# Gate and residual folded into the output accumulation, the final norm read from PSUM, and both scatters of the former pair ahead of the transposes

## The reference, cut to what matters

```python
    for l in range(DEPTH):
        ...
        h = rms_norm(x, ffn_norm_g[l]) * (1.0 + scale_f) + shift_f
        ffn = moe_ffn(h, ...)          # routed experts + shared expert
        x = x + gate_f * ffn
    return rms_norm(x, final_norm_g)

    # in moe_ffn, per chunk of tokens:
        a = jnp.einsum('td,edf->tef', tc, w1)
        b = jnp.einsum('td,edf->tef', tc, w3)
        hid = jax.nn.silu(a) * b * gc[:, :, None].astype(tc.dtype)
        return jnp.einsum('tef,efd->td', hid, w2)
    shared = jnp.einsum('tf,fd->td', jax.nn.silu(t @ sw1) * (t @ sw3), sw2)
```

## Time and profile before

| | us |
|---|---|
| median of 3 runs | 802.24 |
| lowest and highest | 800.73, 805.15 |
| the profiled execution | 803.2 |
| its span, first to last instruction | 801.4 |
| PE busy, of the span | 731.0 (91%) |
| DVE busy | 284.4 (35%) |
| ACT busy | 175.5 (22%) |
| HBM read and written | 269.51 MB and 1.05 MB |

### The profile page before, as it was taken

How to read it: one execution, slowest core, us unless ns; L and a number is a source line. 1 busy time by engine, 2 the same in 40 slices (tenths; PEclk the granted TensorE clock), 3 DMA queues, 4 the chain that set the end, 5 groups by cost and what they waited for, 6 DMA issues and landing times.

```text
span 801.4 us, 12516 instructions
## 1 busy us (share of the span) xinstructions
PE 731.0 (91%) x5004; PEld 384.2 (48%) x5004; DVE 284.4 (35%) x750; ACT 175.5 (22%) x351; POOL 10.6 (1%) x25
## 2 busy tenths in 40 slices
PE   4699999999998988999997999999999997999991
PEld 1478888888885444333332333333333333333330
DVE  1118493855546484212221222221222222222225
ACT  3213320200000333212121212121212222212122
POOL 0200001000000010000000000000000000000000
PEclk9899999999999999999999999999999999999996
DMA  9999526695959253999999999999999999999951
GB/s 337 372 340 366 171 95 220 227 326 174 359 208 421 85 236 123 422 422 420 421 420 418 422 420 422 420 421 395 413 418 422 419 421 419 421 420 421 420 216 52
DMA packets 73429, 271.37 MB, mean 339 GB/s; under 512 B 4424, under 2 KB 33232, under 8 KB 48416
## 3 DMA queue, kind: packets, MB, share of 16 engines
q1 hardware_dynamic: 71664, 264.26, 84.0%
q0 software_dynamic: 1408, 6.20, 2.0%
q10 hardware_dynamic: 304, 0.13, 0.1%
HBM read 269.51 MB, written 1.05 MB: 338 GB/s over the span
## 4 chain that ended last, share of the span: by engine, by line
PE 81%; DVE 9%; ACT 3%; DMA 3%; issue 2%; SPq 2%; DVEq 0%; ACTq 0%
PE bank L1087 78%; DVE slot_gate L1034 2%; PE bank L1398 2%; DVE reg L1038 2%; DMA ring<-ada_w_dram 2%; DVE reg L1029 2%; ACT reg L618 2%; SPq L356 1%; DMA reg<-reg 1%; ACT h_hT L603 0%; DVE x_sb L1070 0%; DVE part L1069 0%; DVE part L738 0%; DVE h_hT L1078 0%; ACT h_hT L646 0%
## 5 line engine op out<-in xcount | busy, mean ns | idle before, releaser
L1087 PE MATMUL bank<-ring,h_hT 128*32 128x512 f32 (+2 forms) x2144 | 256.3, 590 | 7.4 <-issue 7.4
L1087 PEld LDWEIGHTS bank<-ring,h_hT 128*32 128x32 f32 (+1 forms) x2144 | 84.5, 114 | 169.2 <-issue 167.5
L1087 PE MATMUL bank<-h_hT,ring 128*128 128x256 f32 x704 | 157.6, 383 | 1.8 <-ACT h_hT L464 1.8
L1087 PEld LDWEIGHTS bank<-h_hT,ring 128*128 128x128 f32 x704 | 135.0, 192 | 21.3 <-ACT h_hT L464 2.2
L1087 PE MATMUL bank<-ring,turned 128*32 128x512 f32 x1024 | 116.5, 595 | 0.0
L1029 DVE TENSOR_TENSOR reg<-reg,bank 128x256 f32<-128x256 f32 x32 | 13.5, 421 | 212.9 <-ACT reg L618 212.9
L1050 DVE TENSOR_TENSOR y_part<-bank,y_part 128x512 fp32r<-128x512 f32 x64 | 44.2, 691 | 123.9 <-ACT y_part L629 91.1
L1087 PEld LDWEIGHTS bank<-ring,turned 128*32 128x32 f32 x1024 | 30.0, 109 | 69.1 <-issue 69.1
L618 ACT ACTIVATE reg<-bank 128x256 f32<-128x256 f32 x32 | 12.3, 384 | 220.3 <-PE bank L1087 220.3
L1087 PE MATMUL bank<-y_part,give 64*128 64x512 f32 (+1 forms) x268 | 49.4, 443 | 2.3 <-DVE y_part L1050 1.5
L1087 PE MATMUL bank<-take,h_part 128*128 128x256 f32 x288 | 50.6, 300 | 0.7 <-ACT h_hT L603 0.7
(11 more groups left out here) (221 smaller groups left out, 415.6 us busy)
## 6 DMA issues: line engine op xcount, KB each, us to landing
ring<-exp_w_dram SPq DMA_DIRECT2D x192, 1024.0 KB, 13.0
ring<-ada_w_dram SPq DMA_DIRECT2D x24, 1024.0 KB, 12.1
ring<-w_in_dram SPq DMA_DIRECT2D x24, 1024.0 KB, 12.8
ring<-w_branch_dram SPq DMA_DIRECT2D x4, 1024.0 KB, 12.4
ring<-w_out_dram SPq DMA_DIRECT2D x4, 1024.0 KB, 8.1
ring<-shared_w_dram SPq DMA_DIRECT2D x2, 1024.0 KB, 13.8
reg<-ada_bp_dram POOLq DMA_DIRECT2D x3, 512.0 KB, 8.6
x_sb<-x_dram SPq DMA_DIRECT2D x1, 1024.0 KB, 5.3
```

What stands on the lines that cost most here:

```text
L1087: return pe.matmul(o, lhsT, rhs, start=start, stop=stop, skip_group_check=True)
```

## The change

Three things are done.

1. **The gate.** `gate_f` is multiplied into the shared expert's w2 once, on DVE ahead of the loop (two operations of 128 x 1024), and into y of each pair, on DVE, in place in banks 6 and 7 (two operations of 128 x 512 a pair), before ACT copies it. ACT now waits for that (`y_gated`).
2. **The residual and the norm.** Four matmuls of the identity with `x_sb`, between the two loops, add x into the output banks. Behind the loop ACT squares the output banks themselves (with the factor 1/32 inside the square, so that the mean needs no further multiply), and DVE scales from the banks. The eight DVE operations of gate and residual are gone, and one of the three small ones of each norm. A root of one unused column is put on ACT right behind the loop, ahead of the squares.
3. **The scatters.** `scatter(1 - r, 1)` now stands right behind `scatter(1 - r, 0)`, ahead of the transposes.

```diff
@@ ACT, in the body
-                    act.wait_ge(S["y0_done"], n + 1)
+                    act.wait_ge(S["y_gated"], 2 * n + 1)
                     act.activation(y_part[0][:, 0:512], bank[B_Y[0]][:, :], ACT.Copy).then_inc(S["y_top"], 1)
-                    act.wait_ge(w2_used[r], step + 1)
+                    act.wait_ge(S["y_gated"], 2 * n + 2)
                     act.activation(y_part[0][:, 512:D], bank[B_Y[1]][:, :], ACT.Copy).then_inc(S["y_top"], 1)
@@ ACT, behind the loop
+            act.activation(rstd[:, 4:5], rstd[:, 5:6], ACT.Sqrt).then_inc(S["a_step"], 1)
             for tb in range(TB):
-                for k in (2 * tb, 2 * tb + 1):
-                    cols = slice((k % 2) * 512, (k % 2 + 1) * 512)
-                    act.wait_ge(S["x3_done"], k + 1)
-                    act.activation(h2[:, tb, cols], x_sb[:, tb, cols], ACT.Square, accum_out=ssq[:, k:k + 1])\
-                       .then_inc(S["x3_sq"], 1)
+                for hf in range(2):
+                    act.wait_ge(S["sum_done"], hf + 1)
+                    act.activation(h2[:, tb, hf * 512:(hf + 1) * 512], bank[B_OUT[2 * tb + hf]][:, :], ACT.Square, scale=1.0 / 32,
+                                   accum_out=ssq[:, 2 * tb + hf:2 * tb + hf + 1]).then_inc(S["x3_sq"], 1)
@@ DVE, ahead of the loop
             cast_out(7)
+            dve.wait_ge(S["cast_read"], 8)
+            dve.wait_ge(S["sw2_in"], 16)
+            for j in range(2):
+                dve.tensor_tensor(shared_w2[:, j * D:(j + 1) * D], shared_w2[:, j * D:(j + 1) * D], gate_f, ALU.mult)\
+                   .then_inc(S["sw2_gated"], 1)
@@ DVE, behind the loop
-                    link(dve.tensor_tensor(gb2, bank[B_OUT[k]][:, :], gate_f[:, cols], ALU.mult))
-                    dve.tensor_tensor(x_sb[:, tb, cols], x_sb[:, tb, cols], gb2, ALU.add).then_inc(S["x3_done"], 1)
@@ PE, in the body
                     scatter(1 - r, 0)
+                    scatter(1 - r, 1)
                     pe.wait_ge(S["hid_done"], n + 1)
...
                     gather(1 - parity, 2 * gm + 1)
-                    scatter(1 - r, 1)
                     pe.wait_ge(S["turn_read"], n + 1)
@@ PE, between the loops
-            pe.wait_ge(S["sw2_in"], 16)
+            for k in range(4):
+                tb, hf = k // 2, k % 2
+                mm(bank[B_OUT[k]][:, :], ident, x_sb[:, tb, hf * 512:(hf + 1) * 512], False, False)
+            pe.wait_ge(S["sw2_gated"], 2)
             pe.wait_ge(S["sh_TT"], 1)
```

More of the change, by code:

```diff
@@ L289, in decoder_layer @@
             take_built pair_gates gate_mm slot_gated gathered gath_read sig1_done th_done hid_done turn_done turn_read
-            give_read y0_done y_top y_split pos_next sum_done x3_done x3_sq x3_var x3_rstd fin_done stored""".split()
+            sw2_gated give_read y0_done y_gated y_top y_split pos_next sum_done x3_sq x3_var x3_rstd fin_done stored""".split()
         S = {n: sem(n) for n in names}
@@ L1047, in body @@
                     for hf in range(2):
+                        if hf:
+                            dve.wait_ge(w2_used[r], use * (BODY_PAIRS // 2) + m // 2 + 1)
+                        else:
+                            dve.wait_ge(S["y0_done"], n + 1)
+                        dve.tensor_tensor(bank[B_Y[hf]][:, :], bank[B_Y[hf]][:, :], gate_f[:, hf * 512:(hf + 1) * 512], ALU.mult)\
+                           .then_inc(S["y_gated"], 1)
+                    for hf in range(2):
                         cols = slice(hf * 512, (hf + 1) * 512)
@@ L1061, in _ @@
             for tb in range(TB):
[L1062 to L1068, removed]
-                    link(dve.tensor_tensor(gb2, bank[B_OUT[k]][:, :], gate_f[:, cols], ALU.mult))
-                    dve.tensor_tensor(x_sb[:, tb, cols], x_sb[:, tb, cols], gb2, ALU.add).then_inc(S["x3_done"], 1)
                 dve.wait_ge(S["x3_sq"], 2 * tb + 2)
-                link(dve.tensor_tensor(rstd[:, 8 + tb:9 + tb], ssq[:, 2 * tb:1 + 2 * tb], ssq[:, 1 + 2 * tb:2 + 2 * tb], ALU.add))
-                link(dve.tensor_scalar(rstd[:, 8 + tb:9 + tb], rstd[:, 8 + tb:9 + tb], 1.0 / D, EPS, ALU.mult, ALU.add))
+                link(dve.tensor_scalar(rstd[:, 8 + tb:9 + tb], ssq[:, 2 * tb:1 + 2 * tb], ssq[:, 1 + 2 * tb:2 + 2 * tb], EPS,
+                                       ALU.add, ALU.add))
                 dve.reciprocal(rstd[:, 8 + tb:9 + tb], rstd[:, 8 + tb:9 + tb]).then_inc(S["x3_var"], 1)
@@ L1077, in _ @@
                     cols = slice(hf * 512, (hf + 1) * 512)
-                    dve.scalar_tensor_tensor(out=h2[:, tb, cols], in0=x_sb[:, tb, cols], scalar=rstd[:, 10 + tb:11 + tb],
+                    dve.scalar_tensor_tensor(out=h2[:, tb, cols], in0=bank[B_OUT[2 * tb + hf]][:, :], scalar=rstd[:, 10 + tb:11 + tb],
                                              in1=final_g[:, cols], op0=ALU.mult, op1=ALU.mult).then_inc(S["fin_done"], 1)
```

## The result

The median of five runs is **795.95 us** (793.91 to 796.42), against 802.51 for the kernel before in five runs beside it: a ratio of 0.991 with an interval of 0.989 to 0.993. A second set of runs of the same kernel gave 795.42, ratio 0.991 (0.989 to 0.993). 795.5 was predicted, from 792.5 to 799.5. The profiled execution took 795.1 us, its span is 793.3; before they were 803.2 and 801.4.

A forecast was written before the change was run, and what follows sets the result against it. The prediction took the loop as good as bound by DMA's weight loads, with a chain of DVE and ACT operations behind it. Last pair -0.6 and tail -6.1 gave -6.7 us: from 802.24 to 795.5, range 792.5 to 799.5.

The forecast's parts named there:

- The bound of the loop: Loop as good as bound by DMA; of PE's 19 us only the last pair's 0.6 us remain.
- Rival (a): DMA is not at its limit and PE's 19 us come through: time near 780; chance 0.03.
- The scatter: In each pair, second scatter fits PE's gap before the transposes: 0.6 us a pair saved, period 13.6.
- Pair 15 at the landing, 527.8: PE gains 1.7 us by pair 15, whose hidden stage then starts as its weights land, at 527.8.
- The residual: Four matmuls between the loops: net 2.7 us later, 32.4 from pair 15's start to next w1/w3 issue; costs nothing.
- The dip: DMA rate falls between the loops, 1.7 us lost; grows by 0.3 to 0.4 and takes pair 31's landing with it.
- rival (b): The dip in DMA vanishes and the hand-overs shrink: 793.4; chance 0.14.
- (c): Dip grows or pair 31 meets a late landing (+2.7), one slow stage (+1.7), or tail gives less: 798.2 to 800; chance 0.17.
- The gates: Gate on shared expert's w2 costs nothing; gate in the body nothing in pairs 0 to 30, +0.8 us in pair 31.
- The norm: Tail behind the loop: last scaling done at 792.8 instead of 798.88, -6.1 us with the gate's +0.8 in it.
- The sum: Whole kernel: -0.6 (last pair) -6.1 (tail) = -6.7 us, giving 795.5 from 802.24.
- Rival (d), the clock: PE's waits for weights make the clock fall, slowing the stages of pairs 30 and 31: 808.3; chance 0.04.

The follow-up runs named there:

- half-bytes pair: Changed kernel and kernel before, each with every expert load cut to its first half (changed kernel: from pair 2 on): 784.81 us and 800.81 us.
- The scatter alone: Kernel before with only the second scatter moved ahead of the transposes; gate, residual and norm as before: 801.70 us, ratio 0.998.
- residual first, no jump: Changed kernel with identity matmuls behind pair 7, first two bodies written out, and the four bank-zeroing matmuls ahead of the loop gone: 793.66 us.

## Why the prediction was right, point by point

**The bound of the loop.** Right, and it is the step that carried the forecast. Read from slices at 421 GB/s and margins of 1.7 and 0.3 us, it said that of PE's gain only the last pair's would remain. The half-bytes pair of runs shows it: 784.8 for after, 800.8 for before. Rival (a), 780, is what half the bytes come near to, and what full bytes don't allow. Pair 31 was to start within 1 us of 769.6; it did in the second profile (770.15), and in the first it was 1.25 early, 0.89 of which is the start of pair 0.

**The scatter.** The mechanism was right, its size a little off. 0.6 us a pair was said, a period of 13.6; it is 0.45 and 13.77. The step that was off took the w2 stage to start when `turned` is ready (about 765.5 for 765.45). In the loop it starts 0.22 us behind. Where the bodies are written out it does start 0.06 behind, and the period there is the 13.59 that was said, so 0.16 is PE's own issue inside the loop and no hand-over. Nothing hung on it in the loop, and the last pair gave 0.44 instead of 0.6. For the same reason the waits for weights were 0.8 to 1.1 us and not 1.3, and came in pairs 13 to 15 and 29 to 31 and not from 11 and 27 on.

**Pair 15 at the landing, 527.8.** It started at 526.66 with a wait of 1.07; 0.89 of the difference is the earlier start of pair 0. The scatter alone, with the old start, has 527.60.

**The residual.** 32.4 us from pair 15 to the next issue were said; it is 558.95 - 526.66 = 32.29. The dip was to grow by 0.3 to 0.4: by the arithmetic of the prediction it is (422 - 388 + 422 - 419) / 422 x 20 = 1.8 us in the first profile of after and 2.5 in the second (379 and 413), where 1.7 stood, and 1.0 without the four matmuls. So it grew by 0.1 and 0.8. But it does not go over to pair 31 one to one, as the prediction took it: 0.7 to 1.4 us less of it moved pair 31 by 0.2 to 0.3 against pair 15. Why so little is open. Neither rival (b), the dip gone, nor the +2.7 of (c) came.

**The gates.** That on w2 of the shared expert left no trace in the path: its two operations took 2.36 us, up to 309.67, and DVE was idle until 317.11. In the body, a gate on a bank in place is 0.70 us (x64 in the page), so a write to a bank isn't dearer than one elsewhere. In pair 31 the last scatter came 784.57 - 782.38 = 2.19 behind the first gate; 2.29 was said.

**The norm.** 11.2 us from the last w2 stage to the end of the span were said, 10.9 were measured, in both profiles of after and in the run without the scatter's move. The 0.3 lie in the squares: they start 0.59 us apart (785.34, 785.93), for the read of the sum of the first runs beside the second square, where I had put 0.73 for each from the earlier trace rows. The extra root ended at 785.22, 0.12 ahead of the first square; the margin was said as 0.3. A gain of only 5.0 in the tail, by a drain, did not come.

**The sum.** -6.7 was said. The medians give 802.51 - 795.95 = 6.56, and the two profiles of after 8.1 and 6.3. That it is so near is in part luck: the last pair gave 0.16 too little and the tail 0.3 too much, and the start of pair 0, which no term of the sum holds, moves a single profile by 1.1.

**Rival (d), the clock.** The waits of 0.8 to 1.1 us for weights did no harm: every stage behind one took 7.07 or 7.08, also behind the 1.96 us of residual first, no jump (464.87). The kernel that the Trainium skill (TensorE: Matmul & The Clock Gate, HAM oscillation) tells of, with each burst left cold by a wait, waited about 3 to 5 us each time; the waits here were shorter, and the prediction was wrong to take it for the same case. What was slow was behind the two jumps, 2.6 and 2.7 us, and the supply hid both. Rival (c) had one slow stage of 1.7 in its price and would have had it right only where PE is the bound, as in the kernel without the scatter's move.

**Open.** Why pair 0 starts at 309.56 in some profiles and 310.6 in others. The granted clock in the window from 32 to 40 us goes with it in most: it is 0.79 in the first profile of after and 0.69 in the second, and 0.69 in before, and 0.59 in the one that starts pair 0 last, at 311.25. But the kernel without the extra root has 0.79 there and starts pair 0 at 310.59, so this window doesn't settle it.

## What to carry to other kernels

Count what an engine saves only up to the margin of the resource beside it, and read that margin at the last stage, as the landing of its data against its start; beyond the margin a saving turns into a wait, and a cost of the same size beside it becomes free, so that parts of a change have no price of their own. Where loads bound a loop, time is to be had at its two ends: ask for the first reload sooner (1.1 us here, up to pair 30), begin the last stage on the half of its data that comes first (1.8), and shorten what stands behind it (6.4). In such a tail take each operation off the chain, and put what has no input, such as a table load, under another engine's work.

## What the runs showed of the hardware

PE stands still for 3.4 to 3.9 us at every jump back of this loop, and not at all where the bodies are written out. A long queue of loads doesn't make it longer: in after a load issued at the start of the first pause lands 18.3 to 21.2 us later, with half the bytes 3.8 to 5.0 us later, and still the pauses there are 3.38 and 3.89 (3.75 and 3.61 in before with half the bytes). That busy DMA engines have no part in it is not shown: their share is 0.70 over the 100 us above, but 0.93 and 0.95 in the two pauses. The Trainium skill (Runtime: NRT & Kernel Launch, Instruction fetch mechanics) says that a taken branch to a page that isn't held must wait for its fetch, and the trace agrees in that the pause goes with the jump; the fetch itself stands in no row here. Behind such a pause the first stage took between 7.07 and 10.71 us, at a granted clock of 1.00 in the quick ones and 0.72 to 0.75 in those above 9.6, and nothing I found tells which it will be.

Matmuls of 256 columns cost half of those of 512 (128 in 7.11 us, 64 in 7.07), so a stage may be cut in two for the order of its data at a price of about 0.04 us. ACT's read of a sum from one square runs beside the next square, 0.59 us from start to start.
